# Five groups of projections with the activations as the stationary operand and 512 weight columns streaming, in a hybrid SSD and attention layer

## The reference, cut to what matters

```python
h      = rms_norm(x, mix_norm_w)
z, xbc, dt, q, k, v, g_ssm, g_att = split(h @ w_in)     # 256 x 2048 @ 2048 x 20544
b_ssm  = mamba2_branch(z, xbc, dt) @ w_ssm_proj         # 4096 -> 2048
b_att  = diff_attention(q, k, v) @ w_attn_proj          # 2048 -> 2048
x      = x + (S(g_ssm) * b_ssm + S(g_att) * b_att) @ w_out
h      = rms_norm(x, ffn_norm_w)
a      = silu(h @ w_ffn_gate) * (h @ w_ffn_up)          # 2048 -> 5632, twice
x      = x + a @ w_ffn_down                             # 5632 -> 2048
```

## Time and profile before

| | |
|---|---|
| median of three runs | 2181.34 us (2179.87 to 2187.02) |
| span of the profiled execution | 2180.0 us |
| TensorE busy | 2163.7 us, 99% |
| VectorE busy | 1265.7 us, 58% |
| ScalarE busy | 1017.2 us, 47% |
| DMA read from HBM | 387.24 MB, 179 GB/s over the span |

### The profile page before, as it was taken

The page is one execution under the profiler, slowest core; times in us unless marked ns, Lnnn a source line. Parts: engine busy times, 40 slices in busy tenths (PEclk is TensorE's granted clock), DMA queues, the critical chain, the costliest instruction groups (busy, mean ns, idle before and its releaser), DMA issues.

```text
span 2180.0 us, 38469 instructions
## 1 busy us (share of the span) xinstructions
PE 2163.7 (99%) x14801; PEld 2003.1 (92%) x14801; DVE 1265.7 (58%) x1408; ACT 1017.2 (47%) x1280; POOL 135.6 (6%) x165
## 2 busy tenths in 40 slices
PE   9999999999999999999999999999999999999999
PEld 8888889989999888888999999899999999998887
DVE  6676445555766777777654555555555555554443
ACT  5444444555446555555553333453433434443332
POOL 1111000000001222222000000000000000000000
PEclk9999999999999999999999999999999999999999
DMA  6656755544566555555565555566566665656664
GB/s 220 206 179 208 203 166 149 150 136 141 161 191 193 177 179 173 177 179 177 171 213 189 179 183 189 187 176 183 177 188 182 183 183 173 192 184 202 195 203 142
DMA packets 206331, 394.63 MB, mean 181 GB/s; under 512 B 15602, under 2 KB 20387, under 8 KB 205747
## 3 DMA queue, kind: packets, MB, share of 16 engines
q1 hardware_dynamic: 203778, 385.00, 58.0%
q0 software_dynamic: 2336, 8.46, 1.2%
q10 hardware_dynamic: 144, 0.20, 0.0%
HBM read 387.24 MB, written 2.16 MB: 179 GB/s over the span
## 4 chain that ended last, share of the span: by engine, by line
PE 93%; DVE 3%; issue 3%; ACT 1%; DMA 0%; DVEq 0%; SPq 0%; ACTq 0%
PE acc L1271 55%; PE acc L1257 31%; PE side L1359 2%; DVE w_lo L723 2%; PE side L1287 2%; PE side L1481 1%; DVE conv_x L833 1%; PE side L1362 0%; DVE yT L1002 0%; ACT w_hi L412 0%; PE side L1487 0%; DMA rows<-in_subln_w 0%; PE side L1435 0%; PE side L1377 0%; PE side L1379 0%
## 5 line engine op out<-in xcount | busy, mean ns | idle before, releaser
L723 DVE TENSOR_TENSOR w_lo<-w_raw,w_hi 128x1024 fp32r<-128x1024 f32 x712 | 901.3, 1273 | 778.4 <-ACT w_hi L412 774.5
L412 ACT ACTIVATE w_hi<-w_raw 128x1024 fp32r<-128x1024 f32 x712 | 751.1, 1058 | 1006.4 <-PE acc L1271 629.6
L1271 PE MATMUL acc<-x2T_hi,w_hi 128*128 128x256 f32 x1408 | 398.6, 283 | 0.0
L1271 PE MATMUL acc<-x2T_hi,w_lo 128*128 128x256 f32 x1408 | 398.5, 283 | 0.0
L1271 PE MATMUL acc<-x2T_lo,w_hi 128*128 128x256 f32 x1408 | 398.5, 283 | 0.0
L1271 PE MATMUL acc<-h_hi,w_hi 128*128 128x256 f32 x1280 | 371.9, 291 | 0.0
L1271 PE MATMUL acc<-h_lo,w_hi 128*128 128x256 f32 x1280 | 362.6, 283 | 0.0
L1271 PE MATMUL acc<-h_hi,w_lo 128*128 128x256 f32 x1280 | 362.5, 283 | 0.0
L1271 PEld LDWEIGHTS acc<-x2T_lo,w_hi 128*128 128x128 f32 x1408 | 270.3, 192 | 0.0
L1271 PEld LDWEIGHTS acc<-x2T_hi,w_hi 128*128 128x128 f32 x1408 | 270.3, 192 | 0.0
L1271 PEld LDWEIGHTS acc<-x2T_hi,w_lo 128*128 128x128 f32 x1408 | 270.3, 192 | 0.0
(11 more groups left out here) (226 smaller groups left out, 2776.5 us busy)
## 6 DMA issues: line engine op xcount, KB each, us to landing
w_raw<-in_w_in SPq DMA_DIRECT2D x320, 512.0 KB, 4.0
w_raw<-in_w_ffn_gate SPq DMA_DIRECT2D x88, 512.0 KB, 3.7
w_raw<-in_w_ffn_up SPq DMA_DIRECT2D x88, 512.0 KB, 4.0
w_raw<-in_w_ffn_down SPq DMA_DIRECT2D x88, 512.0 KB, 4.2
w_raw<-in_w_ssm_proj SPq DMA_DIRECT2D x64, 512.0 KB, 4.0
w_raw<-in_w_attn_proj SPq DMA_DIRECT2D x32, 512.0 KB, 4.3
w_raw<-in_w_out SPq DMA_DIRECT2D x32, 512.0 KB, 4.2
acs_b<-acs_scratch POOLq DMA_DIRECT2D x16, 512.0 KB, 5.9
```

Source lines behind the costliest of these rows:

```text
L412: nc.scalar.activation(w_hi[:, r], w_raw[:, r], ACT.Copy).then_inc(hi_ready, 1)
L723: nc.vector.tensor_tensor(w_lo[:, r], w_raw[:, r], w_hi[:, r].bitcast(F32), ALU.subtract).then_inc(lo_ready, 1)
L1271: done = nc.tensor.matmul(out_at, w[:, r, kk, cut], a[:, k0 + kk], start=first and kk == n == 0 and c % 2 == 0, stop=last and kk == UK - 1 ...
```

## The change

The attention's gate, the attention projection, the SSM's gate, the SSM projection and the FFN's gate and up products go from `cols_unit` to `rows_unit`. The tiles `merge_a`, `gate_s`, `m_row`, `gate_f` and `up_f` now have tokens on partitions. The merged branches and the FFN's product are transposed on TensorE, 8 transposes to each 512 columns, and ScalarE and VectorE take hi and lo from `side`. As tokens are on partitions, 1/rms is a scalar for each partition; `rstd_b`, `diag` and their matmuls are gone. The loops over the SSM projection and the down product are written out on TensorE.

```diff
@@ tensor engine
-                        chunk(cols_unit, c, h_hi, h_lo, between=heads_between(i * 4 + (8 * n + 2 * c)))
+                        chunk((cols_unit, rows_unit)[n], c, h_hi, h_lo, between=heads_between(i * 4 + (8 * n + 2 * c)))
...
-                    chunk(cols_unit, c, ya_hi, ya_lo, between=last_heads)
+                    chunk(rows_unit, c, ya_hi, ya_lo, between=last_heads)
...
-                chunk(cols_unit, c % 2, h_hi, h_lo, between=between)
+                chunk(rows_unit, c % 2, h_hi, h_lo, between=between)
+            def merged_columns(c):
+                pe.wait_ge(m_ready, c + 1)
+                if c:
+                    pe.wait_ge(m_lo_ready, c)
+                else:
+                    pe.wait_ge(yT_ready, G)
+                to_columns(m_row, 0).then_inc(m_T, 1)
+            def ssm_between(c):
+                def between(u):
+                    if c and u == 3:
+                        merged_columns(c - 1)
+                return between
             pe.wait_ge(y_lo_ready, KI // 4)
-            with repeat(pe, 2, [(unit, 4 * UPC), (pair, 1)]) as i:
-                for c in range(2):
-                    chunk(cols_unit, c, y_hi, y_lo, 2 * UPC)
+            for c in range(D // CW):
+                chunk(rows_unit, c % 2, y_hi, y_lo, 2 * UPC, between=ssm_between(c))
...
             def out_between(c):
                 def between(u):
+                    if c == 0 and u == 2:
+                        merged_columns(3)
...
-                if u == 7:
-                    pe.wait_ge(diag_ready, 1)
-                        last = nc.tensor.matmul(side[:, 0, t * P:(t + 1) * P], ones[:], diag[:, t], start=True, stop=True)
-                    last.then_inc(rstd_T, 1)
+            def products_columns(i, head):
+                pe.wait_ge(a_ready, i + 1)
+                if not head:
+                    pe.wait_ge(a_lo_ready, i)
+                for n in range(CT):
+                    for t in range(TT):
+                        at_col = (n % 2) * T + t * P
+                        last = transpose(side[:, n // 2, at_col:at_col + P], up_f[:, t, n * P:(n + 1) * P])
+                last.then_inc(a_T, 1)
+            def gate_between(i, head):
+                def between(u):
+                    if u == 2:
+                        products_columns(i, head)
+                return between
-                for c in range(2):
-                    chunk(cols_unit, c, x2T_hi, x2T_lo)
+                chunk(rows_unit, 0, x2T_hi, x2T_lo, between=gate_between(i + 1, False))
+                chunk(rows_unit, 1, x2T_hi, x2T_lo)
...
             def last_ffn(u):
+                if u == 2:
+                    products_columns(FF // CW - 1, False)
@@ vector engine, merging: now one chunk later, after split_lo of u == 4 (c > 0), or u == 3 of the first w_out chunk
+            def merged_lo(c):
+                dve.wait_ge(m_hi_ready, c + 1)
+                nc.vector.tensor_tensor(m_lo[:, cut], side[:, 2:4].rearrange("p b (n t) -> p (b n) t", t=T),
+                                        m_hi[:, cut].bitcast(F32), ALU.subtract).then_inc(m_lo_ready, 1)
@@ vector engine, FFN
-                nc.vector.tensor_tensor(gate_f[:], sums(0), rstd, ALU.mult).then_inc(gate_f_scaled, 1)
...
+                    if not head and u == 3:
+                        product_lo(i - 1)
...
-                link(nc.vector.tensor_tensor(up_f[:], sums(1), rstd, ALU.mult))
-                nc.vector.sem_inc(acc_free[1], 1)
-                nc.vector.tensor_tensor(up_f[:], up_f[:], gate_f[:], ALU.mult).then_inc(a_ready, 1)
-                nc.vector.tensor_tensor(a_lo[:, cut], up_f[:], a_hi[:, cut].bitcast(F32), ALU.subtract).then_inc(a_lo_ready, 1)
+                for t in range(TT):
+                    last = nc.vector.scalar_tensor_tensor(out=up_f[:, t], in0=acc[1][:, t], scalar=x2_scale[:, t:t + 1],
+                                                          in1=gate_f[:, t], op0=ALU.mult, op1=ALU.mult)
+                last.then_inc(a_ready, 1)
@@ scalar engine, FFN: gate_silu stands at the end of the gate chunk, product_hi after split_hi of u == 2
+                for t in range(TT):
+                    last = nc.scalar.activation(gate_f[:, t], acc[0][:, t], ACT.Silu, scale=x2_scale[:, t:t + 1])
+                last.then_inc(gate_f_ready, 1)
+            def product_hi(i):
+                act.wait_ge(a_T, i + 1)
+                nc.scalar.activation(a_hi[:, bass.ds(i * CT, CT)], side[:, 0:2].rearrange("p b (n t) -> p (b n) t", t=T),
+                                     ACT.Copy).then_inc(a_hi_ready, 1)
```

More of the change, by code:

```diff
@@ L647, in _, with merged_hi @@
                 chunk_done()
-                nc.scalar.activation(gate_s[:, c * CT:(c + 1) * CT], sums(c % 2), ACT.Sigmoid).then_inc(acc_free[c % 2], 1)
-            with repeat(act, 2, [(unit, 4 * UPC)]) as i:
-                for c in range(2):
[L653 to L656, removed]
+                nc.scalar.activation(gate_s[:, c], acc[c % 2][:], ACT.Sigmoid).then_inc(acc_free[c % 2], 1)
+            def merged_hi(c):
+                act.wait_ge(m_T, c + 1)
+                nc.scalar.activation(m_hi[:, c * CT:(c + 1) * CT], side[:, 2:4].rearrange("p b (n t) -> p (b n) t", t=T),
+                                     ACT.Copy).then_inc(m_hi_ready, 1)
+            for c in range(4):
+                for u in range(2 * UPC):
+                    split_hi()
+                    if c and u == 3:
+                        merged_hi(c - 1)
             def residual_hi(c):
@@ L690, in ffn_pair @@
                         nc.scalar.activation(x2_sq[:, t], x2[:, t], ACT.Square, accum_out=x2_sums[:, t:t + 1]).then_inc(x2_ss, 1)
-                    if head and u == 7:
-                        act.wait_ge(rstd_T, 1)
-                        nc.scalar.activation(rstd_b[:], side[:, 0, 0:T], ACT.Copy).then_inc(rstd_b_ready, 1)
+                    if not head and u == 2:
+                        product_hi(i - 1)
+                chunk_done()
+                gate_silu(i, head)
                 for u in range(UPC):
                     split_hi()
-                    if u == 1:
-                        gate_silu(i)
-                up_hi(i)
             ffn_pair(0, True)
@@ L1082, in _ @@
                         nc.vector.tensor_tensor(y_lo[:, cut], yT[:, cut], y_hi[:, cut].bitcast(F32), ALU.subtract).then_inc(y_lo_ready, 1)
-            with repeat(dve, 2, [(unit, 4 * UPC), (own, 2)]) as i:
-                for c in range(2):
[L1087 to L1095, removed]
+            def merged_lo(c):
+                dve.wait_ge(m_hi_ready, c + 1)
+                cut = slice(c * CT, (c + 1) * CT)
+                nc.vector.tensor_tensor(m_lo[:, cut], side[:, 2:4].rearrange("p b (n t) -> p (b n) t", t=T),
+                                        m_hi[:, cut].bitcast(F32), ALU.subtract).then_inc(m_lo_ready, 1)
+            for c in range(4):
+                for u in range(2 * UPC):
+                    split_lo()
+                    if c and u == 4:
+                        merged_lo(c - 1)
+                chunk_done()
+                if c:
+                    dve.wait_ge(m_T, c)
+                link(nc.vector.tensor_tensor(m_row[:], acc[c % 2][:], gate_s[:, c], ALU.mult))
+                nc.vector.sem_inc(acc_free[c % 2], 1)
+                nc.vector.tensor_tensor(m_row[:], m_row[:], merge_a[:, c], ALU.add).then_inc(m_ready, 1)
             def residual_lo(c):
@@ L1110, in _ @@
                     split_lo()
+                    if c == 0 and u == 3:
+                        merged_lo(3)
                     if c and u == 4:
@@ L1156, in _ @@
                     split_lo()
+                    if c == 0 and u == 3:
+                        product_lo(FF // CW - 1)
                 dve.wait_ge(mm_done, unit.now(0 if final else -LEAD))
@@ L1602, in _ @@
             pe.wait_ge(a_lo_ready, FF // CW - 1)
-            with repeat(pe, 2, [(unit, KF), (pair, 1)]) as i:
-                for c in range(2):
-                    chunk(rows_unit, c, a_hi, a_lo, KF // UK, between=last_ffn)
+            chunk(rows_unit, 0, a_hi, a_lo, KF // UK, between=last_ffn)
+            chunk(rows_unit, 1, a_hi, a_lo, KF // UK)
+            chunk(rows_unit, 0, a_hi, a_lo, KF // UK)
+            chunk(rows_unit, 1, a_hi, a_lo, KF // UK)
 def kernel(**inputs):
```

86 lines of the change are left out of this document (43 added, 43 removed).

## The result

The changed kernel takes 2145.24 us (median of four runs, 2143.6 to 2146.78) against 2180.75 us before; the ratio is 0.9834 (95% interval 0.9822 to 0.9846). 2142 was forecast, in a range from 2135 to 2151. The time of the profiled run is 1.7 us more than its span (2146.78 against 2145.1), where I had taken 1.3. By spans the change gave 2180.0 - 2145.1 = 34.9 us, and the sum had said 39.5. So 4.6 us are missing.

A forecast was written before the change was run, and what follows sets the result against it. TensorE was taken to bound the kernel, by matmul count times spacing plus what stands between units. Terms -53.8 - 0.7 + 13.4 + 1.1 + 0.5 = -39.5 us on 2180.0 gave 2140.5, as median 2142; range 2135 to 2151.

The forecast's parts named there:

- (a): Five groups changing form: 336 units each gain 0.16 us on TensorE by halving their matmuls, 53.8 us.
- (b): Before the FFN: the four removed matmuls of ones with diag save 0.7 us on TensorE.
- (c): Merged branches and FFN product: 15 added blocks of eight transposes at 0.89 us cost 13.4 us.
- (f): Merging: m_row is ready before TensorE's transposes need it, with 3.0 us or more to spare; cost nothing.
- (g): FFN product: a_ready comes 4.4 us before TensorE asks for it; cost nothing, with 0 to 5 us kept in reserve.
- (h): Weights: a 512 KB unit every 2.72 us instead of 2.88, as the down product already does; cost nothing.
- Rival 2: Merging or FFN: a_ready or free side late by 1 or 2 us per block, 2157 or 2172; 0.09 with costly clock falls.
- rival 3: Converted units: fixed share not per matmul, 2196 (chance 0.03); by the skill page's 2.5 ns rule, 2186 (0.02).
- rival 4: FFN: a_ready 13 us after the chunk's end stops TensorE 4.8 us at 11 blocks, 53 us, 2195; chance 0.01.
- rival 1: Clock: one fall more or fewer, at most 1.7 us (within forecast's 0.84); costly, behind 15 blocks, 2167 (within a shared 0.09).
- (d): Small matmuls between converted units: about 37 places at 0.03 us more cost 1.1 us, bounds 0 and 3.3.
- (e): Attention gate: fixed chain for the second head turns some gain into waiting, 0.5 us, between 0.3 and 5.1.

The follow-up runs named there:

- the experiment with 256 columns: Changed kernel with each 512-column matmul of the FFN's gate and up done as two of 256, activations still stationary: 2172.76 us.
- the table loads back: Changed kernel with the attention gates' sigmoid moved to the attention projection, plus an unused one-column sigmoid after each copy of the gates: 2146.15 us.

## Why the prediction held, and the step that was too small

- (a) Units: 336 x 0.16 = 53.8 us was right as a price per matmul, as the experiment with 256 columns confirms. The attention projection's stage fell by 5.1 us (5.12 forecast), gate and up by 19.7 for 20.0.
- (b) and (c): right. The FFN alone gave 18.95 us for a forecast of 19; the blocks cost 0.89 us each in the trace, and 0.85 by the medians (0.87 by the trace) when doubled.
- (f), (g), (h): right, no wait in the merging and the FFN. Silu's two parts take 1.27 us (1.2 forecast); the table load of 1.28 us in front of the first, which (g) left out, cost TensorE nothing. Rival 2, rival 3 with the form by the page, rival 4 and rival 1's costly form (a fall behind each block) did not occur.
- (d) Small matmuls beside rows units: forecast 1.1 us for all 37 places, and 1.0 for the 32 in the gate stage. Measured there without waits and clock: 5.1 - 2.6 = 2.5 us, nearly all of what the upper bound of 0.09 a place allows for 32 (2.9). So this term was 1.5 us too small. By the starts of the units in the two kernels with the late sigmoid, most units gained 0.08 to 0.13 us where 0.16 was forecast, and seven gained nothing. Four of these seven are the sixth unit of each gate chunk, 3.60 to 3.61 us in the columns form and 3.61 in the rows form (3.71 once). There the gap between the last big matmul and the second head's values was 0.12 us, the pitch of the columns form, and is 0.30 in the rows form (0.40 once) against a pitch of 0.23. This fits an input that comes through ScalarE at a fixed time; I tested it no further.
- (e) The attention gate: the term that was most mis-sized. For the waits alone "I take 0.5 us" was a little too much, since they grew by only 0.2 to 0.3 us. Their effect on the clock was put into rival 1, at "at most 1.7 us" for one more fall, and left out of the sum. In the profiled runs there were 6.83 us more at half clock, twice what rival 1 allowed. By the stage's times the clock cost (138.20 - 131.50 - 2.3) = 4.4 us in the changed kernel and (137.58 - 134.10 - 2.1) = 1.4 us before, so 3.0 us.

Together: 1.5 us in (d) and 3.0 in the clock, less the 0.3 that the waits cost less than forecast, make the 4.2 us of the gate stage. The other 0.4 us of the 4.6 lie elsewhere, 0.3 of them in gate and up, unexplained. As medians the forecast missed by 3.2 us, and since each median mixes runs with more and with less half clock, a part of the miss is chance.

Not settled: why such a wait is followed by 3.41 or 6.83 us at half clock in one run and by none in another. Its length alone does not decide: behind the filling, rests of 0.31 us had no fall, and a wait of 0.27 us with the table loads back had one. Seven of the ten profiles, that of before among them, also have 3.41 us at half clock within the first 16 us, and the changed kernel's has none; its first big matmul starts at 17.25 us against 17.44 before, so this is worth about 0.2 us of the comparison.

## What to carry to other kernels

Where TensorE bounds a kernel, count matmuls as well as columns: the pitch (the time from one start to the next) is here columns at 2.4 GHz plus 13.3 ns, so the operand with more columns should stream, as long as the transposes that this needs (0.89 us for 8) stay below the 1.28 us that a chunk of eight units gains. A stage whose chain of small steps is as long as the big work beside it gains less from shorter big work (2.6 of 5.1 us here, with the waits for the exponentials gone); look for its waits first, and for the clock behind them. In the profiled run of the changed kernel the waits behind the exchanges of ScalarE's table, and the clock behind the waits, cost 6.7 us, more than the conversion of that stage could bring. Moving one sigmoid out of the way gave 5.4 us in the changed kernel, and 1.6 in the kernel before.

## What the hardware showed that I had not expected

- Waits of TensorE of 0.27 to 0.98 us amid small matmuls were followed 1.5 to 3.2 us behind their end by a granted clock of 0.50 for 3.41 or 6.83 us, in some runs and not in others. Filling the wait with six rows of small matmuls (0.83 us) kept it at 1.00 in the stage of the profiled run.
- The fixed share of a matmul with its load is 13.3 ns, at 256 columns whichever operand stands still, and at 512 columns with the activations standing still; weights standing still with 512 columns were not run.
- Eight transposes of 128x128 in a row cost 0.79 us, and eight more right behind them 0.87.
